# Plain fp32 matmuls instead of three fp32r passes, and up projections computed feature-major, in a two-block transformer kernel

## The reference

```python
def first_block(x, c, ...):
    c_act = jax.nn.silu(c)
    for i in range(DEPTH):                      # DEPTH = 2
        mod = c_act @ w_mod[i] + b_mod[i]       # 1024 x 6144, six sections
        sh1, sc1, g1, sh2, sc2, g2 = jnp.split(mod, 6, axis=-1)
        h = modulate(rmsnorm(x, norm_mix[i]), sh1, sc1)
        y = pool_mixer(h, ...) if i == 0 else moba_attention(h, w_qkv, w_o, rel_bias)
        x = x + g1[:, None, :] * y
        h = modulate(rmsnorm(x, norm_mlp[i]), sh2, sc2)
        x = x + g2[:, None, :] * squared_relu_mlp(h, w_up[i], w_down[i])   # 1024 -> 4096 -> 1024
    return rmsnorm(x, norm_final)

def squared_relu_mlp(h, w_up, w_down):
    a = jax.nn.relu(h @ w_up)
    return (a * a) @ w_down
```

## Time and profile before

| | |
|---|---|
| median of 3 runs | 1230.55 us (1228.34 to 1230.89) |
| span of the profiled execution | 1229.1 us, 14350 instructions |
| PE | 1098.8 us busy (89%), 5513 matmul records |
| PEld | 927.8 us (75%) |
| DVE | 681.5 us (55%), of it 314.0 us the weight subtractions of line 1049 |
| ACT | 451.5 us (37%), of it 267.9 us the weight copies of line 557 |
| POOL | 109.6 us (9%) |
| HBM read | 193.76 MB, mean 159 GB/s |
| granted PE clock | 0.892 of full speed on average |

### The profile page before, as it was taken

The page is one execution under the profiler, slowest core; times in us unless marked ns, Lnnn a source line. Parts: engine busy times, 40 slices in busy tenths (PEclk is TensorE's granted clock), DMA queues, the critical chain, the costliest instruction groups (busy, mean ns, idle before and its releaser), DMA issues.

```text
span 1229.1 us, 14350 instructions
## 1 busy us (share of the span) xinstructions
PE 1098.8 (89%) x5513; PEld 927.8 (75%) x5513; DVE 681.5 (55%) x1074; ACT 451.5 (37%) x748; POOL 109.6 (9%) x108
## 2 busy tenths in 40 slices
PE   5489999999799898899999879999869689999995
PEld 5488777777698688678888669986659677777774
DVE  5487666776645894544444366623373545554453
ACT  1113433433444321444444345542222334443342
POOL 2000100101000000010010010001074000000000
PEclk9976999999799657899999869985679988999998
DMA  9876577677354653154454513540000023545510
GB/s 342 286 271 228 211 253 266 208 270 271 140 206 151 206 192 138 71 200 160 185 196 177 188 47 131 203 137 1 1 1 1 19 85 103 183 159 191 185 68 34
DMA packets 105178, 195.47 MB, mean 159 GB/s; under 512 B 2283, under 2 KB 46572, under 8 KB 105132
## 3 DMA queue, kind: packets, MB, share of 16 engines
q1 hardware_dynamic: 104380, 192.58, 44.6%
q0 software_dynamic: 752, 2.26, 0.5%
HBM read 193.76 MB, written 1.07 MB: 159 GB/s over the span
## 4 chain that ended last, share of the span: by engine, by line
PE 70%; DVE 16%; ACT 5%; issue 5%; DMA 3%; POOL 1%; SPq 1%; DVEq 0%; ACTq 0%; POOLq 0%
PE ps L1593 16%; PE ps L1632 12%; PE ps L1661 10%; PE ps L1858 6%; DVE wl L1049 5%; PE ps L1749 4%; DMA raw<-in_w_mod 3%; PE ps L2077 3%; DVE arena L909 2%; PE ps L1543 2%; ACT wh L557 2%; DVE arena L936 2%; PE ps L1993 1%; ACT arena L574 1%; PE ps L1762 1%
## 5 line engine op out<-in xcount | busy, mean ns | idle before, releaser
L1049 DVE TENSOR_TENSOR wl<-raw,wh 128x1024 fp32r<-128x1024 f32 (+1 forms) x288 | 314.0, 1135 | 306.1 <-ACT wh L557 305.8
L557 ACT ACTIVATE wh<-raw 128x1024 fp32r<-128x1024 f32 (+1 forms) x288 | 267.9, 982 | 364.6 <-PE ps L1593 135.1
L1593 PE MATMUL ps<-wh,H 128*128 128x512 f32 x288 | 117.5, 408 | 6.1 <-DVE L L1032 3.3
L1593 PE MATMUL ps<-wl,H 128*128 128x512 f32 x288 | 116.2, 403 | 0.0
L1593 PE MATMUL ps<-wh,L 128*128 128x512 f32 x288 | 115.4, 401 | 0.0
L1661 PE MATMUL ps<-wh,aTh 128*128 128x512 f32 x256 | 103.2, 403 | 8.9 <-DVE wl L1049 8.9
L1632 PE MATMUL ps<-wh,H 128*128 128x512 f32 x256 | 103.4, 404 | 2.4 <-DVE wl L1049 2.4
L1661 PE MATMUL ps<-wl,aTh 128*128 128x512 f32 x256 | 102.7, 401 | 0.0
L1661 PE MATMUL ps<-wh,aTl 128*128 128x512 f32 x256 | 102.5, 400 | 0.0
L1632 PE MATMUL ps<-wl,H 128*128 128x512 f32 x256 | 101.4, 396 | 0.0
L1632 PE MATMUL ps<-wh,L 128*128 128x512 f32 x256 | 101.2, 395 | 0.0
(11 more groups left out here) (373 smaller groups left out, 1943.2 us busy)
## 6 DMA issues: line engine op xcount, KB each, us to landing
raw<-in_w_up SPq DMA_DIRECT2D x16, 2048.0 KB, 7.5
raw<-in_w_down SPq DMA_DIRECT2D x16, 2048.0 KB, 7.7
raw<-in_w_mod SPq DMA_DIRECT2D x12, 2048.0 KB, 9.7
raw<-in_w_in SPq DMA_DIRECT2D x7, 2048.0 KB, 7.5
raw<-in_w_mod SPq DMA_DIRECT2D x12, 1024.0 KB, 7.5
raw<-in_w_qkv SPq DMA_DIRECT2D x6, 2048.0 KB, 10.9
raw<-in_w_mod SPq DMA_DIRECT2D x8, 1536.0 KB, 7.0
raw<-in_w_gate SPq DMA_DIRECT2D x11, 1024.0 KB, 5.3
```

The source lines that it names most:

```text
L557: e.activation(dst, src, ACT.Copy).then_inc(S["split_h"], 1)
L1049: e.tensor_tensor(o, src, i1.bitcast(F32), ALU.subtract).then_inc(S["split_l"], 1)
L1593: ins = e.matmul(ps[:, bank, :], src[xa][:, 4 * hb + k, META + P * m:META + P * m + P], w[wb][:, k, :], start=(hb == 0 and k == 0 and n == 0),
```

## The change

`wh`, `wl`, `H`, `L`, `aTh`, `aTl` and both helpers called `split` are gone (their memory is kept as work space for later tensors). Every big projection reads `raw` and `hf` directly, with one plain fp32 matmul where three fp32r matmuls stood. A slot of `raw` is now free only when PE has used its tile (`tile_used`, `w_used`).

`up` and `g_up` are feature-major: 128 weight columns are the stationary operand and the 256 tokens move. Their result lies as `down` needs it, so `turn`, `g_turn` and the splits of the activations are gone; relu and the square write `act[buf]`, which now has two buffers. `down` still moves 512 weight columns.

Two things move. The pool weights lie in slot 0 until the pool matmuls have read them, and the load of modulation unit 7 (and SP's later ones) waits for that. The first `wo` tile is now loaded behind the modulation units of the attention stage, no longer before them. In MLP0, PE's last `gate_mm(4)` stands directly behind the last modulation sum, and DVE makes its diagonals (`gate_diag`) only after that sum's columns.

```diff
-        wh = sb("wh", [P, 2, HALF], F32R)
-        wl = sb("wl", [P, 2, HALF], F32R)
+        sb("work_w", [P, 2 * SLOT])
...
-            def free_split(t):
-                e.wait_ge(S["split_l"], 4 * t + 4)
+            def tile_used(t):
+                e.wait_ge(S["w_used"], 2 * t + 2)
...
                 if u == 7:
-                    free_split(T_POOL)
+                    tile_used(T_POOL)
                 load_mod0(u)
...
-            for i in range(1, 7):
-                free_split(T_QKV + i - 4)
-                src = wqkv[:, :, 512 * i:512 * i + 512] if i < 6 else wo[:, :, 0:512]
-                load((N_QKV + i) % R, kview((N_QKV + i) % R), src)
+            for i in range(1, 6):
+                tile_used(T_QKV + i - 4)
+                load((N_QKV + i) % R, kview((N_QKV + i) % R), wqkv[:, :, 512 * i:512 * i + 512])
             for u in range(NMU):
                 if u < R:
-                    free_split(T_QKV + 3 + u)
+                    tile_used(T_QKV + 2 + u)
                 else:
                     e.wait_ge(S["mod_accu"], u - R + 1)
                 s = (N_MOD1 + u) % R
                 load(s, raw[:, s, 0:KD * MUW].rearrange("p (k n) -> p k n", k=KD),
                      wmod[1][:, :, 3 * D + MUW * u:3 * D + MUW * u + MUW])
             e.wait_ge(S["mod_accu"], 5)
+            load(N_WO % R, kview(N_WO % R), wo[:, :, 0:512])
...
+            with e.Fori(2, 8) as j:
                 mod_halves(j)
-                split(T_MLP0 + 1 + 2 * j, 2)
                 mod_cols1(j)
-                mlp_aT(j)
-            mod_halves(7)
             nch[0] += 14 * 6
-            split(T_MLP0 + 14, 3)
             gate_diag(modc[:, 0, 40:48])
-            mod_cols1(7)
-            mlp_aT(7)
-            split(T_MLP0 + 15, 0)
             gate_copy(1, 4)
             e.wait_ge(S["mod_col"], 18)
             scale_cols(2, 1, 104, 1)
...
+            def rows_half(hb, b, name, slot):
+
+                w = kview(slot)
                 for m in range(NM):
                     bank = b(m) if callable(b) else b + m
-                    for k in range(4):
-                        parts(4 * hb + k)
-                        for n, (xa, wb) in enumerate(PASSES):
-                            ins = e.matmul(ps[:, bank, :], src[xa][:, 4 * hb + k, META + P * m:META + P * m + P],
-                                           w[wb][:, k, :], start=(hb == 0 and k == 0 and n == 0),
-                                           stop=(hb == 1 and k == 3 and n == 2))
+                    for k in range(4 * hb, 4 * hb + 4):
+                        parts(k)
+                        ins = e.matmul(ps[:, bank, :], hf[:, k, META + P * m:META + P * m + P], w[:, k, :],
+                                       start=(k == 0), stop=(k == KD - 1))
                     if hb == 1 and m == 0:
                         ins.then_inc(S[name], 1)
                 return ins
...
+            def up(it, slot, land):
+
+                e.wait_ge(raw_in[slot], land)
+                w = kview(slot)
+                for b in range(2):
+                    if not (isinstance(it, int) and it == 0):
+                        e.wait_ge(S["a_done"], 2 * it - 1 + b)
+                    for c in range(2):
+                        f0 = 256 * b + P * c
+                        for k in range(KD):
+                            parts(k)
+                            ins = e.matmul(ps[:, 4 + b, SEQ * c:SEQ * c + SEQ], w[:, k, f0:f0 + P], hf[:, k, META:TT],
+                                           start=(k == 0), stop=(k == KD - 1))
+                    ins.then_inc(S["w_used"], 1)
+
+            def down(it, buf, slot, land, last=False):
+
+                e.wait_ge(S["a_done"], 2 * it + 2)
+                e.wait_ge(raw_in[slot], land)
+                w = dview(slot)
                 for hb in range(2):
                     for m in range(NM):
                         for c in range(2):
+                            for k in range(2 * hb, 2 * hb + 2):
+                                ins = e.matmul(ps[:, 2 * m + c, :], act[buf][:, k, P * m:P * m + P],
+                                               w[:, k, 512 * c:512 * c + 512], start=False, stop=(last and k == 3))
                             if last and hb == 1 and 2 * m + c < 3:
                                 ins.then_inc(S["y_done"], 1)
+                    ins.then_inc(S["w_used"], 1)
...
-            up(0, T_MLP0)
-            turn(0)
-            up(1, T_MLP0 + 1)
-            down(0, T_MLP0 + 2)
-            e.wait_ge(S["r_done"], 4)
+            fresh[0] = 1
+            up(0, *landed(N_MLP0))
+            up(1, *landed(14))
+            down(0, 0, *landed(15))
             e.wait_ge(S["mod_acc"], 11)
             e.wait_ge(S["mod_accb"], 1)
             for c in range(8):
-                ins = e.matmul(ps[:, 5, c:c + 1], acc[:, c // 4, P * (c % 4):P * (c % 4) + P], ones[:, 0:1],
+                ins = e.matmul(ps[:, 6, c:c + 1], acc[:, c // 4, P * (c % 4):P * (c % 4) + P], ones[:, 0:1],
                                start=True, stop=True)
             ins.then_inc(S["mod_mm"], 2)
-            turn(1)
-            with e.Fori(2, 8) as j:
-                up(j, T_MLP0 - 1 + 2 * j, 10 + j)
-                down(j - 1, T_MLP0 + 2 * j)
-                e.wait_ge(S["r_done"], 2 * j + 2)
-                e.wait_ge(S["mod_acc"], 10 + j)
-                e.wait_ge(S["mod_accb"], j)
-                for c in range(4):
-                    ins = e.matmul(ps[:, 5, c:c + 1], acc[:, c // 2, P * (c % 2):P * (c % 2) + P], ones[:, 0:1],
-                                   start=True, stop=True)
-                ins.then_inc(S["mod_mm"], 1)
-                turn(j)
+            with e.Fori(1, 4) as i:
+                for r in range(2):
+                    j = 2 * i + r
+                    up(j, 2, 16 * (3 + j))
+                    down(j - 1, 1 - r, 3, 16 * (3 + j))
+                    e.wait_ge(S["mod_acc"], 10 + j)
+                    e.wait_ge(S["mod_accb"], j)
+                    e.wait_ge(S["mod_col"], 10 + j)
+                    for c in range(4):
+                        ins = e.matmul(ps[:, 6, c:c + 1], acc[:, c // 2, P * (c % 2):P * (c % 2) + P], ones[:, 0:1],
+                                       start=True, stop=True)
+                    ins.then_inc(S["mod_mm"], 1)
             e.wait_ge(S["mod_col"], 18)
+            e.wait_ge(S["r_done"], 16)
             gate_mm(4)
-            down(7, T_MLP0 + 15, last=True)
+            down(7, 1, *landed(40), last=True)
...
+            def g_up(j, slot, land):
+                e.wait_ge(raw_in[slot], land)
                 if not (isinstance(j, int) and j == 0):
+                    e.wait_ge(S["ga_done"], j)
+                w = kview(slot)
+                for b in range(2):
+                    for c in range(2):
+                        f0 = 256 * b + P * c
+                        for k in range(KD):
+                            parts(k)
+                            ins = e.matmul(ps[:, 4 + b, SEQ * c:SEQ * c + SEQ], w[:, k, f0:f0 + P], hf[:, k, META:TT],
+                                           start=(k == 0), stop=(k == KD - 1))
+                    ins.then_inc(S["w_used"], 1)
```

More of the change, by code:

```diff
@@ L242, in before, with g_slot @@
             return 16 * len([i for i in range(N_FFN) if i % R == n % R])
+        def g_slot(n, i=0):
+            seen = sum(2 if (k - N_FFN == 0 or (k - N_FFN) % 2 == 1) and k != N_FFN + 21 else 1
+                       for k in range(N_FFN, n + 1) if k % R == n % R)
+            step = 32 if (n - N_FFN) % 2 == 1 else 16
+            return n % R, before(n) + 16 * seen + step * i
         def kview(s):
@@ L836, in _ @@
                              ).then_inc(S["on_sq"], 1)
-                if m == 0:
-                    e.wait_ge(S["s1_mm"], 1)
-                    split(T_WOUT, *landed(N_WOUT))
             to_hf()
-            split(T_WOUT + 1, *landed(N_WOUT + 1))
             stats(0, [(S["r2_add"], 2), (S["r2_add"], 4)])
-            split(T_FFN, N_FFN % R, before(N_FFN) + 32, qs=(0, 1))
             to_hf(pcol[:, 1, 24:32])
-            split(T_FFN, N_FFN % R, before(N_FFN) + 32, qs=(2, 3))
-            def g_silu(j, t):
-                for m in range(NM):
-                    e.wait_ge(*((S["gu_done"], j + 1) if m == 0 else (S["split_used"], 2 * t + 2)))
-                    e.activation(relu[:, m, 0:256], ps[:, 4 + m, 0:256], ACT.Silu).then_inc(S["gr_done"], 1)
@@ L854, in g_aT @@
-            def g_aT(j):
-                e.wait_ge(S["gt_done"], j + 1)
-                e.activation(aTh[:, 0:2, :], ps[:, 6, :].rearrange("p (k t) -> p k t", k=2), ACT.Copy).then_inc(S["gth_done"], 1)
-            def g_slot(n, i=0):
-                seen = sum(2 if (k - N_FFN == 0 or (k - N_FFN) % 2 == 1) and k != N_FFN + 21 else 1
-                           for k in range(N_FFN, n + 1) if k % R == n % R)
-                step = 32 if (n - N_FFN) % 2 == 1 else 16
-                return n % R, before(n) + 16 * seen + step * i
```

(48 more changed lines are left out.)

450 lines of the change are left out of this document (113 added, 337 removed).

## The result

The changed kernel takes 1341.81 us (median of four runs, 1338.15 to 1344.7) against 1230.72 for the kernel before on the same chip: a ratio of 1.092, with a 95% interval from 1.088 to 1.096. It is 111 us slower. The forecast was 1359 us with a range from 1335 to 1408. The profiled execution has a span of 1343.0 us against 1229.1, so 113.9 us are to be found in it.

What follows compares the result with a forecast made beforehand. PE was taken to bound the kernel, busy 89% of the span, mostly in big projection passes. Stage shifts summed to +128.8 us on a span of 1229.1, 1357.9; with 1.45 for the runs, 1359 us, range 1335 to 1408.

Steps and rivals of the forecast that it cites:

- The price: All big projections: a plain record costs 0.222, 0.236 or 0.437 us for 256, 272 or 512 columns, 930 us in all.
- the estimate of 1337 us: Whole kernel: time if every plain record cost N/2.4 + 2.5 ns, the skill's gap for isolated matmuls.
- Waits and gaps: Whole kernel: waits and gaps give back 43 us, beside the 19 of the transposes.
- the middle stage: Second attention and delta rule: untouched, but the split ahead of WOUT's second normalisation goes, -3.0 us.
- the start: Before MLP0: unit 7's load is issued at about 80 us instead of 60; +0.5 us, bounds 0 to +3.
- then PE needs about 7 us a unit: Before MLP0: after beginning unit 7 at 87.5, PE takes about 7 us a modulation unit, as long as the next load.
- rival C: MLP0: modulation loads land over 5 us later, PE waits in six iterations, 3 us each give 1377 us; 12%.
- Attention: Attention stage: stays as it is, 3.58 us a head; starts 1.7 us earlier, `wo_out` 1.15 earlier.
- A: Big projections: a long plain matmul costs two cycles a column in all, kernel faster, about 1035 us; 3%.
- B: Plain matmuls: weight loads are exposed, 0.08 us for each of 1640 matmuls, +131, 1490 us; 5%.
- D: Plain passes: PE's clock stays at 1.2 GHz, all 930 us double, near 2290 us; 2%.
- E: Weight splits: held back more than counted; all 86 us and the transposes leave the chain, 1316 us, still slower; 4%.

Runs made afterwards that it cites:

- run 1: Kernel before with a fourth fp32r pass, low part by low part, in each big projection; splits and transposes stay: 1452.09 us, ratio 1.181.
- run 4: Kernel after with the down matmuls cut into pieces of 256 columns in MLP0 and 128 in MLP1: 1342.6 us in one execution.
- run 8: Kernel before with three passes over the high parts alone and VectorE's subtraction for the weights cut to 8 columns: 1194.92 us in one execution.
- run 7: Kernel after with GpSimd's eight scalings in the delta rule held back until VectorE's ten are done: 1332.49 us, ratio to the kernel before 1.0844.
- run 6: Kernel after with the pool weights in a place of their own, so unit 7's load need not wait: 1339.33 us, ratio to the kernel before 1.0896.
- run 5: Kernel after run again unchanged, as the measure for two small changes to it: 1336.06 us, ratio to the kernel before 1.0885.
- run 2: Kernel before with three fp32r passes and splits, but both MLPs' up projections feature-major without transposes of their activations: 1225.36 us, ratio 0.999.
- run 3: Kernel after with MLP1's up projection back in token-major form, plain fp32, with the transposes: 1352.6 us, ratio to the kernel before 1.0995.

## Why the prediction was right, and where it was off

- *Sign and mechanism.* The step that decided was the cost of a plain record, two for each matmul and two cycles a column each, read from short matmuls at both clocks. The long records confirm it, and run 1 shows that a fourth cycle a column is enough for the whole loss.
- *The price.* The forecast's term was too high: 0.222, 0.236 and 0.437 us taken, 0.216, 0.229 and 0.429 measured, which is below even the low bounds of 0.218, 0.232 and 0.432. With the forecast's counts that is 908 us in place of 930, 22 us of the miss. The bounds took the 5 ns on top of L2022 for a record's own. But L2022 has 128 columns, and run 4 shows that such a record ends at a floor of 0.112 us, above its columns: its 5 ns were the floor, and longer records have 2.5. The high bounds also put the fp32r pass's 18 ns on 213 on the plain record, and the prices taken lie a sixth to under a third of the way towards them; runs 4 and 8 show that the 18 ns belong to the fp32r pass.
- The Trainium skill's rule (page "TensorE: Matmul & The Clock Gate", section "Back-to-back issue gap") of N/2.4 + 2.5 ns is given there for isolated matmuls. It agrees with the plain records of MLP1's `up`, WIN and `down` to 0.1 ns if N is put at twice the columns; the estimate of 1337 us that the prediction worked out from it would have been the better forecast. It does not hold at 128 columns (0.1116 us against 0.1092, run 4), and for fp32r passes it is short by 9 to 16 ns at the full clock.
- *Waits and gaps.* The forecast gave back 43 us. Read: 908 - 739 - 19 is 150, the span grew by 113.9, so 36 came back, 7 fewer. With the price taken out, the stages miss with both signs: MLP0 +2.1, the FFN +1.9, the middle stage +2.8 and the start +1.7, `wo_out` -1.5 and WOUT -1.1, the rest under 1. Two of them have a cause. The middle stage kept its length (-0.2 instead of -3.0): the splits ahead of WOUT went, but VectorE's 6.76 us scaling took their place, a turn of the contention that run 7 shows. And the first MLP0 matmul came 2.2 us late instead of 0.5, within the bound of 3. The load of unit 7 did what was forecast: it was issued at 79.4 us, and PE, idle for 2.6 us, began the unit with it at 87.2, where the forecast had 87.5. What failed is "then PE needs about 7 us a unit": the next unit began 9.25 us later, behind this wait:

```profile
96.46 5.25 PE L1322 MATMUL ps<-ccol,raw 128*128 128x1 f32 x24 [2.26 <-DVE modc L806]
```

  The next unit's load, held back with unit 7's, landed at 92.6 us, and VectorE sums 3.6 us of it before it makes the columns that PE waits for. The scatter of this event over the runs is larger than the miss (run 6).
- *MLP0.* No PE wait stands before the modulation matmuls (0.79 us, touching both neighbours in the chain above): rival C did not come. The iteration was 28.44 us against 29.1, all of it price. Its `up` takes 13.92 us, 0.1 more than the same 64 records in MLP1; what that is stays open.
- *Attention* kept 3.58 us a head, and QKV to `wo_out` shifted by 12.5 us against 14.1, price again.
- *The rivals.* A: a long plain matmul costs 0.43 or 0.86 us, four cycles a column. B: at most 2.4 ns a record, and at 128 columns only. D: granted clock 0.98 to 1.00 in the plain stages. E: run 8 puts VectorE's part of the splits at some 30 us and run 1 shows some 19 us covered by one more pass, so they are about what the forecast held, not 86. (The 86 were read from shares rounded up; by the finer 4.7 and 1.5% of the chain they are 76.)
- Price -22 and waits +7 are the -15 between +128.8 and +113.9; that a third of the price's miss was cancelled by the waits is luck. The forecast landed 17 us high, 1.3%: the profiled execution is 2.9 us above the median.

## What to carry to other kernels

A plain fp32 matmul is four cycles a column in two records; a product of split operands is three passes of a cycle each. Where PE bounds the kernel, emptying VectorE and ScalarE buys nothing that PE does not wait for, and PE's waits here were some 36 us against 169 us of added records. Before a small difference is explained, compare a stretch that nothing touched: here it moved by 5 to 8 us with the clock (runs 1, 5 and 8). Take apart a change that bundles two ideas: one half of this one added 169 us of records and is the whole loss, the other is worth 0.7 us an iteration where PE is the bound, and nothing or a loss where VectorE is (run 2). To size a long record from short ones, look first whether the short ones stand on a floor.

## What the runs showed of the hardware that was not expected

- At the full clock an fp32r pass has 11 ns over its columns at 256 (11.33 / 96 = 0.118, run 2), 18 ns at 512; a plain record has 2.5 ns at 256, 272 and 512 columns. The 18 ns stay with VectorE's busy time down from 681.5 to 419.5 us (run 8).
- A plain record of 128 columns takes 0.112 us at the full clock with a stationary operand of 128 x 128 (run 4). Eight one-column records of the modulation take 0.89 us in the second execution of the kernel after, 0.111 each, so the columns are not what sets the floor.
- A VectorE operation of 0.67 us took 1.5 us beside GpSimd's tensor operations, and 6.76 us in all five profiled executions of the kernel after and its variants in which GpSimd ran beside it (both of the kernel after, runs 3, 4 and 6).
- The second attention of one kernel ran its heads in 3.27 or 5.84 us, at the granted clock of 1.00 or 0.50, in two executions of it; that is most of the 10.3 us between their spans. The profiled executions of runs 1 and 8 had such a stretch too. And 1.28 us of waiting was followed by 3.4 us at the lower clock in three iterations of run 2, and was not in another.
